# Norm sums partly on GpSimd, and stages that open with four output tiles per operand tile

## The reference, cut to what matters

```python
def modulated_norm(x, g, shift, scale):
    return rms_norm_2(x, g) * (1 + scale) + shift      # x * rsqrt(mean(x^2) + 1e-6) * g
```

```python
def channel_mixer(h, w_up, ffn_dw_w, ffn_dw_b, w_down):
    u = causal_depthwise_conv(h @ w_up, ffn_dw_w, ffn_dw_b)      # 3 taps
    a, b = jnp.split(u, 2, axis=-1)
    return (jax.nn.silu(a) * b) @ w_down
```

## Time and profile before

| | |
|---|---|
| median of 3 runs | 3123.39 us (3120.94 to 3125.38) |
| the profiled execution | 3118.01 us, its span 3116.2 us |
| mean granted TensorE clock | 0.954 of full |
| TensorE busy | 2844.5 us (91%) |
| VectorE, ScalarE busy | 1531.8 us (49%), 1111.8 us (36%) |
| GpSimd busy | 0.2 us |
| DMA | 447.41 MB, mean 144 GB/s |

### The profile page before, as it was taken

One profiled execution on the slowest core, in us unless ns is written; L12 is line 12 of the kernel. 1 busy time (PEld: TensorE's weight loads), 2 busy tenths in 40 slices (PEclk: granted clock), 3 DMA queues, 4 the chain that ended last, 5 costly groups with the idle time before them and its releaser, 6 DMA issues.

```text
span 3116.2 us, 38193 instructions
## 1 busy us (share of the span) xinstructions
PE 2844.5 (91%) x15788; PEld 2328.8 (75%) x15788; DVE 1531.8 (49%) x2262; ACT 1111.8 (36%) x1661; POOL 0.2 (0%) x4
## 2 busy tenths in 40 slices
PE   6887899999868999989999899999989999877998
PEld 4675688997755888977878775787867777655898
DVE  3579636753898357543333423333342323455454
ACT  2444415643444156532222322222232222323443
POOL 0000000000000000000000000000000000000000
PEclk8998899998988999999999999999999999889999
DMA  6541246545421556435353212333225443120553
GB/s 268 195 162 55 75 169 225 214 170 209 157 81 41 189 189 258 170 141 190 121 196 115 81 62 88 128 140 136 105 87 202 151 169 142 68 81 28 189 183 115
DMA packets 122460, 447.41 MB, mean 144 GB/s; under 512 B 13488, under 2 KB 14640, under 8 KB 121904
## 3 DMA queue, kind: packets, MB, share of 16 engines
q1 hardware_dynamic: 122288, 444.97, 39.8%
HBM read 443.87 MB, written 1.05 MB: 143 GB/s over the span
## 4 chain that ended last, share of the span: by engine, by line
PE 78%; DVE 14%; DMA 3%; ACT 3%; issue 1%; SPq 0%; DVEq 0%; ACTq 0%
PE ps L473 21%; PE ps L474 20%; PE ps L475 20%; PE ps L477 17%; DMA ring<-stream 3%; DVE area L1339 3%; DVE area L1515 2%; DVE rests L1263 2%; DVE stat L1370 1%; DVE rs L1302 1%; DVE work L1379 1%; PE ps L637 1%; DVE work L1366 1%; DVE area L1310 1%; ACT heads L925 0%
## 5 line engine op out<-in xcount | busy, mean ns | idle before, releaser
L473 PE MATMUL ps<-h_split,heads 128*128 128x256 f32 (+1 forms) x2992 | 1015.1, 339 | 104.0 <-DVE h_split L1316 60.8
L474 PE MATMUL ps<-h_split,heads 128*128 128x256 f32 (+1 forms) x2992 | 988.6, 330 | 0.0
L475 PE MATMUL ps<-h_split,rests 128*128 128x256 f32 (+1 forms) x2992 | 986.8, 330 | 0.0
L1263 DVE TENSOR_TENSOR rests<-ring,heads 128x1024 fp32r<-128x1024 f32 x520 | 630.2, 1225 | 678.1 <-ACT heads L925 673.2
L925 ACT ACTIVATE heads<-ring 128x1024 fp32r<-128x1024 f32 x520 | 540.6, 1056 | 712.3 <-DMA ring<-stream 370.8
L473 PEld LDWEIGHTS ps<-h_split,heads 128*128 128x128 f32 x2992 | 588.5, 197 | 212.2 <-DVE h_split L1316 69.3
L474 PEld LDWEIGHTS ps<-h_split,heads 128*128 128x128 f32 x2992 | 590.6, 197 | 47.4 <-issue 3.4
L475 PEld LDWEIGHTS ps<-h_split,rests 128*128 128x128 f32 x2992 | 589.1, 197 | 46.1
L473 PE MATMUL ps<-hid_split,heads 128*128 128x256 f32 (+1 forms) x1056 | 365.4, 346 | 0.0
L475 PE MATMUL ps<-hid_split,rests 128*128 128x256 f32 (+1 forms) x1056 | 355.1, 336 | 0.0
L474 PE MATMUL ps<-hid_split,heads 128*128 128x256 f32 (+1 forms) x1056 | 354.8, 336 | 0.0
(11 more groups left out here) (155 smaller groups left out, 2071.4 us busy)
## 6 DMA issues: line engine op xcount, KB each, us to landing
ring<-stream SPq DMA_DIRECT2D x836, 512.0 KB, 3.5
consts<-constants SPq DMA_DIRECT2D x1, 1920.0 KB, 11.3
x_sb<-x_in SPq DMA_DIRECT2D x1, 1024.0 KB, 9.2
x_sb<-ctx_in SPq DMA_DIRECT2D x1, 1024.0 KB, 4.8
out<-area SPq DMA_DIRECT2D x1, 1024.0 KB, 4.8
cols<-columns SPq DMA_DIRECT2D x1, 695.5 KB, 4.1
consts<-constants SPq DMA_DIRECT2D x1, 643.0 KB, 10.3
sg<-positions_in SPq DMA_DIRECT2D x1, 128.0 KB, 10.1
```

The source lines that it names most:

```text
L473: nc.tensor.matmul(out, lhsT[0], rhs[0], start=first, stop=False)
L474: nc.tensor.matmul(out, lhsT[0], rhs[1], start=False, stop=False)
L475: ins = nc.tensor.matmul(out, lhsT[1], rhs[0], start=False, stop=last)
L1263: nc.vector.tensor_tensor(rests[:, u % RING, :], ring[:, u % RING, :], as_f32(heads[:, n % HEADS_RING, :]), ALU.subtract)\
```

## The change

Three things change.

1. GpSimd adds the squares of tiles 1 to 5 of each norm onto tile 0 (`sums`, five additions, each waiting for the one before it). TensorE does three ones-products instead of eight, of the sum and of squares 6 and 7, all after the stage's last output tile.
2. The first four output tiles of `lat`, of each up layer, of `ain` and of `q2` are computed together: four products per k, in four PSUM banks (`linear_quad`). Where a bank held two SEQ tiles, the first four tiles take a bank each (`take_two`), and their readers on ScalarE and VectorE read two banks (`halves_of`). The weight stream is reordered to match (`quad`).
3. In `each_pair` the splits follow the new order: those of pair 2's units stand ahead of `begin(0)`, those of pair 3's units in iteration 0 (on ScalarE between `begin(0)` and `finish(0)`), and iteration 1 has none.

```diff
+SUMMED = KD - 2
@@ weight_blocks
+    def quad(name, n):
+        for k in range(KD):
+            for e in range(4):
+                put(name, k, n + e)
...
             for j in range(lo, hi):
-                pair(up, up_order(width), 2 * j)
+                if lo == 0 and j < 2:
+                    if j == 0:
+                        quad(up, 0)
+                else:
+                    pair(up, up_order(width), 2 * j)
@@ tensor engine
+            def take_two(g):
+
+                if nbank[0] % 2:
+                    nbank[0] += 1
+                b = nbank[0] % BANKS
+                take_bank((*g, "second"), b + 1)
+                take_bank(g, b)
+                nbank[0] += 2
+                return ps[:, b, 0:SEQ], ps[:, b + 1, 0:SEQ]
...
+            def linear_quad(outs, name, n, act, dones, ready):
+
+                for k in range(KD):
+                    ready(k)
+                    for e in range(4):
+                        w, unit = weights(name, k, n + e)
+                        product(outs[e], w, act(k), k == 0, k == KD - 1, dones[e] if k == KD - 1 else None, unit)
...
             def mean_square(p, T_, k):
 
-                if k == 0:
+                if k == SUMMED - 1:
                     for q in last_cols:
 
                         wait_read(q)
                     last_cols[:] = [(p, "ms")]
                     new_banks[(p, "ms")] = COLS_BANK
-                pe.wait_ge(scalar_done, A.at((p, "sq", k)))
-                product(ps[:, COLS_BANK, 0:T_], mat("ones"), squared(T_, k), k == 0, k == KD - 1,
-                        (p, "ms") if k == KD - 1 else None)
-
-            def norm(p, T_, done=0):
-
-                for k in range(done, KD):
+                    pe.wait_ge(pool_done, G.at((p, "sum")))
+                else:
+                    pe.wait_ge(scalar_done, A.at((p, "sq", k)))
+                product(ps[:, COLS_BANK, 0:T_], mat("ones"), squared(T_, 0 if k == SUMMED - 1 else k),
+                        k == SUMMED - 1, k == KD - 1, (p, "ms") if k == KD - 1 else None)
+
+            def norm(p, T_):
+
+                for k in range(SUMMED - 1, KD):
                     mean_square(p, T_, k)
                 return once(lambda k: pe.wait_ge(vector_done, V.at((p, "h", k))))
...
+                def first_pairs():
+                    if shared:
+                        outs = [o for j in range(2) for o in take_two((p, "up", j))]
+                        linear_quad(outs, up, 0, hx, (None, (p, "up", 0), None, (p, "up", 1)), ready)
+                    else:
+                        names = [(p, kind, j) for j in range(2) for kind in kinds]
+                        linear_quad([take_bank(g) for g in names], up, 0, hx, names, ready)
...
                     for j in range(lo, hi):
-                        pair(j, [take_bank((p, kind, j)) for kind in kinds])
+                        if j == 0:
+                            first_pairs()
+                        elif j > 1:
+                            pair(j, [take_bank((p, kind, j)) for kind in kinds])
...
-                        if hi == FJ:
-                            after_down(m)
@@ gpsimd
+            def sums(p, T_):
+
+                for k in range(1, SUMMED):
+                    if k == 1:
+                        pool.wait_ge(scalar_done, A.at((p, "sq", 0)))
+                    pool.wait_ge(scalar_done, A.at((p, "sq", k)))
+                    total = squared(T_, 0)
+                    nc.gpsimd.tensor_tensor(total, total, squared(T_, k), ALU.add)\
+                      .then_inc(pool_done, G.mark((p, "sum") if k == SUMMED - 1 else None))
+                    pool.wait_ge(pool_done, G.n)
@@ scalar engine, each_pair
                     for j in range(lo, hi):
+                        if j == 0:
+                            next_split()
+                            next_split()
                         begin(j)
-                        next_split()
-                        next_split()
+                        if j != 1:
+                            next_split()
+                            next_split()
                         finish(j)
```

More of the change, by code:

```diff
@@ L182, in weight_blocks @@
         if l % 2 == 0:
-            pair("ain", together(range(KD)), 0)
-            linear("ain", KD, range(2, 4))
+            quad("ain", 0)
             linear("uin", KD, range(4))
@@ L380, in bank, with halves_of @@
             return ps[:, bank_of.get(g, 0), :]
+        def halves_of(g, apart):
+            b = bank_of.get(g, 0)
+            return ps[:, b:b + 2, 0:SEQ] if apart else two(ps[:, b, :])
         def as_f32(a):
@@ L573, in hook, with ffn @@
                     pending.append(group)
-            def ffn(p, up, down, T_, ready, after_down):
+            def ffn(p, up, down, T_, ready):
                 shared = T_ == SEQ
@@ L655, in _ @@
                 guests = MIXER_MODS[l]
-                ready = norm((*p, "mix"), SEQ, 0 if l == 0 else KD - 2)
+                ready = norm((*p, "mix"), SEQ)
                 hx = lambda k: h_of(k, slice(0, SEQ))
-                for c in range(3):
-                    out = take_bank((p, "lat", c))
-                    linear(out[:, 0:SEQ], f"lat_{l}", KD, 2 * c, hx, None, ready)
-                    linear(out[:, SEQ:TOK], f"lat_{l}", KD, 2 * c + 1, hx, (p, "lat", c))
+                outs = [o for c in range(2) for o in take_two((p, "lat", c))]
+                linear_quad(outs, f"lat_{l}", 0, hx, (None, (p, "lat", 0), None, (p, "lat", 1)), ready)
+                out = take_bank((p, "lat", 2))
+                linear(out[:, 0:SEQ], f"lat_{l}", KD, 4, hx)
+                linear(out[:, SEQ:TOK], f"lat_{l}", KD, 5, hx, (p, "lat", 2))
                 hook(*guests[0])
@@ L772, in _ @@
                     linear(out[:, 0:SEQ], f"out_{l}", KD, m, lambda k: merged[:, k, :], (p, "out", m))
-                    behind((*p, "ffn"), SEQ)(m)
-                ready = norm((*p, "ffn"), SEQ, KD - 2)
-                ffn((*p, "ffn"), f"up_{l}", f"down_{l}", SEQ, ready,
-                    behind(("b1", 1, "mix"), SEQ) if l == 0 else behind(("b2", 0, "f1"), TOK))
+                ready = norm((*p, "ffn"), SEQ)
+                ffn((*p, "ffn"), f"up_{l}", f"down_{l}", SEQ, ready)
             for l in range(DEPTH):
                 p = ("b2", l)
-                ready = norm((*p, "f1"), TOK, KD - 2)
-                ffn((*p, "f1"), f"f1up_{l}", f"f1down_{l}", TOK, ready, behind((*p, "mix"), TOK))
-                ready = norm((*p, "mix"), TOK, KD - 2)
+                ready = norm((*p, "f1"), TOK)
+                ffn((*p, "f1"), f"f1up_{l}", f"f1down_{l}", TOK, ready)
+                ready = norm((*p, "mix"), TOK)
                 hx = h_of
                 if l % 2 == 0:
-                    linear_pair([take_bank((p, "a", g)) for g in range(2)], "ain", together(range(KD)), 0, hx,
-                                [(p, "a", g) for g in range(2)], ready)
-                    for g in range(2, 4):
-                        linear(take_bank((p, "a", g)), "ain", KD, g, hx, (p, "a", g))
+                    linear_quad([take_bank((p, "a", g)) for g in range(4)], "ain", 0, hx,
+                                [(p, "a", g) for g in range(4)], ready)
                     for g in range(4):
@@ L833, in _ @@
                         linear(take_bank((p, "out", m)), "oab", KD, m, lambda k: mixed[:, k, :], (p, "out", m))
[L834 removed]
                 else:
[L836 removed]
+                    hs = lambda k: h_of(k, slice(0, SEQ))
+                    outs = [o for c in range(2) for o in take_two((p, "q", c))]
+                    linear_quad(outs, "q2", 0, hs, (None, (p, "q", 0), None, (p, "q", 1)), ready)
+                    for c in range(2, 4):
                         out = take_bank((p, "q", c))
[L838 to L839 removed]
+                        linear(out[:, 0:SEQ], "q2", KD, 2 * c, hs)
+                        linear(out[:, SEQ:TOK], "q2", KD, 2 * c + 1, hs, (p, "q", c))
                     for c in range(2):
@@ L876, in _ @@
                         linear(out[:, 0:SEQ], "o2", KD, m, lambda k: attn[:, k, :], (p, "out", m))
-                        behind((*p, "f2"), SEQ)(m)
                 T_ = TOK if l == 0 else SEQ
-                ready = norm((*p, "f2"), T_, KD - 2)
-                ffn((*p, "f2"), f"f2up_{l}", f"f2down_{l}", T_, ready,
-                    behind(("b2", 1, "f1"), TOK) if l == 0 else behind("fin", SEQ))
-            norm("fin", SEQ, KD - 2)
+                ready = norm((*p, "f2"), T_)
+                ffn((*p, "f2"), f"f2up_{l}", f"f2down_{l}", T_, ready)
+            norm("fin", SEQ)
+        @block.gpsimd
+        def _(pool):
+            def sums(p, T_):
[7 more added lines that the diff above has]
+                    pool.wait_ge(pool_done, G.n)
+            for l in range(DEPTH):
+                sums(("b1", l, "mix"), SEQ)
+                sums(("b1", l, "ffn"), SEQ)
+            for l in range(DEPTH):
+                sums(("b2", l, "f1"), TOK)
```

(4 more changed lines are left out.)

48 lines of the change are left out of this document (22 added, 26 removed).

## The result

The changed kernel takes 3098.8 us (median of 4 runs, 3095.1 to 3102.1) against 3122.6 for the kernel before beside it (4 runs, 3120.9 to 3125.4): a ratio of 0.9924, 95% interval 0.9911 to 0.9936, or 23.8 us less. Subtracting the two traces therefore shows only 15.9 of the 23.8 us.

What follows compares the result with a forecast made beforehand. TensorE was taken as the bound, 78% of the chain that ended last. Terms -32.1, -2.5, -8.1, +6.1, +5.7 and +5.2 made 25.7 us less, so the median 3123.4 became 3097.7 us, range 3078 to 3113.

Steps and rivals of the forecast that it cites:

- ones-products: Behind output tiles of ten norms, five products fewer each, 0.43 us in SEQ and 0.85 in TOK: 32.1 us gained.
- quads, five SEQ stages: In `lat` and `up` of both layers and `f2up_1`, four tiles per `h` tile fill TensorE's idle time: 2.5 us gained.
- `q2`: In `q2`, four tiles per k keep TensorE busy and the clock returns sooner: 8.1 us gained, 3.7 if it stays down.
- splits, stall and clock: In `up_0` and `up_1`, moved splits make TensorE stand 6.1 and 5.7 us more, plus 5.2 us for half clock.
- The additions hidden: GpSimd's additions, 0.84 us in SEQ, are covered by output tiles; first norm uncovered: 0, with +1.8 or -4.3 us.
- the fourth rival: GpSimd additions and VectorE's `rests` exclude each other, delaying six norms behind down stages by 42 us: 3140 us, chance 4%.
- The stall: Before the guest's columns, TensorE stands 6.1 us more in `up_0` and 5.7 us more in `up_1`.
- The clock behind it: Behind the stands in `up_0` and `up_1`, 5.2 us of half clock costs 2.6 us each, 5.2 together; bounds 1.7 and 6.3.
- So it isn't repeated: After the stands in `up_0` and `up_1`, ScalarE has a free pair ahead again, so no further stand follows.
- Costless splits: Rival: pair 3's unit lands before ScalarE asks for it, so the moved splits cost nothing: 3080.7 us, chance 18%.
- Costs in all feed-forwards: Rival: copied rows or pair 4's splits come late in the four other feed-forwards too, 6 us each: 3122 us, chance 7%.
- GpSimd as the bound: Rival: the five chained additions outlast six output tiles; gain gone at 4.6 us per SEQ addition, 3147 us at 5; chance 5%.

Runs made afterwards that it cites:

- experiment 2: The kernel before with only GpSimd's sums and three ones-products a norm, matmul order and splits as before: 3093.8 us, ratio 0.9910.
- experiment 4: The changed kernel with `q2` in its old order, one output tile over all k at a time: 3109.2 us, ratio 0.9956.
- experiment 1: The changed kernel with pair 3's two splits back in iteration 1 of each feed-forward: 3081.7 us, ratio 0.9868.
- experiment 7: experiment 1 with three unread additions ahead of each real one, except in the first norm: 3080.4 us, ratio 0.9870.
- experiment 9: The changed kernel with pair 3's splits back in iteration 1, guest's rows copied right behind `begin(j)`, first norm's eight ones-products on TensorE: 3066.7 us, ratio 0.9829.
- experiment 10: experiment 1 with six unread additions ahead of each real one, except in the first norm: 3197.0 us, ratio 1.0240.
- experiment 8: experiment 1 with all eight squares summed by GpSimd, seven additions and one ones-product a norm: 3099.7 us, ratio 0.9931.

## Why the prediction was right

The forecast was 3097.7 us; 3098.8 was measured. The mechanisms were right, but that the time is met within 1.1 us is luck: the errors of the terms cancel. Term by term, each kernel against the kernel before beside it where nothing else is said:

| term | said, us | measured |
|---|---|---|
| ones-products | -32.1 | -27.1 (experiment 2) |
| quads, five SEQ stages | -2.5 | -4.6 (stages of the changed kernel against experiment 2's) |
| `q2` | -8.1 | -7.2 (stage) against before, -8.0 against experiment 4 |
| the two lines above together | -10.6 | -12.1 (experiment 1 against experiment 2) |
| splits, stall and clock | +17.0 | +15.4 (the change against experiment 1; 17.1 between their medians) |
| sum | -25.7 | -23.8 |

The ones-products brought 5.0 less than said, the quads 1.5 more, and the splits cost 1.6 less, each good to 1 or 2 us: in sum the gain is 1.9 too small. Of this the time shows 1.1, as the forecast started from a median of 3123.4 for the kernel before and the one beside the change had 3122.6.

- **Ones-products.** A SEQ product is worth 0.43 as said: `out_0`'s additions lie one bare output tile apart. A TOK one is worth 0.90 rather than 0.85 in the three TOK down stages, each 4.50 us shorter in the trace of experiment 2; behind `down_1` (4.27) and `oab` it is 0.85 to 0.86 as said. That puts the step at about 33. But 0.9 was lost in the first norm, and some 5 us were given back where shorter stages are not what sets the pace. In experiment 2, `up_1` with `down_1` took 0.4 us less than before where 4.3 less was due: TensorE waits 5.8 us for rests where it waited 4.8, 3.7 for rows where it waited 2.0, and works 2.1 us longer at half clock, worth 1.0. `f2up_1` with `f2down_1` took 0.9 us more where 2.1 less was due: the wait for rests, behind a split that waits for its DMA, went from 1.5 to 3.1 us, and the time at half clock from 4.2 to 7.4. So the step that was mis-sized most is this: what is taken from TensorE does not count in full where a wait for the weight stream comes next, because the wait grows. That the transfers might not follow stood among the prediction's signs of being wrong, without a price in the sum.
- **The additions hidden.** Right, 0.76 and 1.29 us on average against 0.84 and 1.7 taken. The ten covered norms have no wait for GpSimd. In the first norm the term said 0 and left out the fourth rival, which is at work there. Here is GpSimd's timeline (the five additions, then the fourth alone), below it VectorE's and TensorE's:

```profile
42.62 4.79 POOL L933 TENSOR_TENSOR sq<-sq 128x256 f32<-128x256 f32 x5 [42.17 <-ACT sq L997]
...
45.03 1.58 POOL L933 TENSOR_TENSOR sq<-sq 128x256 f32<-128x256 f32 x1
```

```profile
44.74 1.29 DVE L1329 TENSOR_TENSOR rests<-ring,heads 128x1024 fp32r<-128x1024 f32 x1 [1.38 <-ACT heads L987]
```

```profile
47.56 2.90 PE L505 MATMUL ps<-sq,consts 128*128 128x256 f32 x6 [4.94 <-POOL sq L933]
```

  The chain ended at 47.4 rather than 46.0: it began at 42.6 rather than 41.8, as everything ahead of it was 0.7 late in this execution, and took 4.8 us rather than 4.2. Four of the additions took 0.72 to 0.73 us; the fourth started while VectorE formed `rests` and took 1.58. That is so in each of the nine traces in which GpSimd adds in this norm. Measured from the last product ahead of it, the root came 0.9 us later than before, and that one addition is 0.86 of it. (The prediction's upper side, +1.8 for additions of 0.42 us, is a slip: 48.91 less 41.8 + 2.1 + 2.6 is 2.4. The lower end of the range, 3078, holds with it: 3080.7 less 2.4 is 3078.3.)
  The Trainium skill (GPSIMD Engine Reference, section "Elementwise — side-by-side cycle accounting") has an addition at 1.96 times VectorE's time, measured there at 2048 columns. The rows give 1.8 at 256 columns (762 ns against the 420 of the earlier trace rows).
- **Quads in SEQ stages.** The direction was right and the size half of what it was. The stages with a quad were 1.4 (`lat_0`), 0.7 (`up_0`), 1.0 (`lat_1`), 0.7 (`up_1`) and 0.8 us (`f2up_1`) shorter than in experiment 2, not 0.5 each. One thing the prediction left out: the clock is back at 1.00 before the last `h` tiles come. In experiment 2 it rises 4.4 us after the first product of `lat_1`, and the seventh step, behind that, still takes 0.67 us where three matmuls at 1.00 take 0.36; idle time there counts in full, not half. The stages behind TOK norms were the same with quads and without (within 0.1 us in experiments 1 and 2), as said, `q2` apart.
- **`q2`.** Right, and by the mechanism said: products without gaps, and the clock back 6.8 us after its fall. The rows of the windows say it, 0.50 to 2714.1 and 1.00 from 2714.3, against 0.50 for 17 us in experiment 4. The Trainium skill (TensorE: Matmul & The Clock Gate, section "Loop structure matters more than you think") wants products back to back and warns of a long wait before every one of them. The trace agrees: 0.50 for 17 us with a wait of some 0.57 us at each `h` tile, and 1.00 again after 6.8 us without.
- **The stall.** The replayed chain was right to a few tenths of a us: from the first split to the columns 15.6 us said, 15.7 measured (493.07 to 508.75). TensorE waits 6.70 in both, against 1.01 and none in the earlier trace rows: 12.4 more, 11.8 said.
- **The clock behind it.** The cost was right, and by luck. The prediction took 5.2 us of half clock at each stand, as behind a norm, worth 5.2 us for both; it lasted 10.0 and 10.2 us. TensorE was busy for 7.15 and 6.82 of these, so each cost half of that, 7.0 for both. But the kernel before had four stretches of 3.4 us at 0.50 around its guests (as experiment 1 has), and the changed kernel has three beside the two long ones. Net it is busy 10.7 us more at half clock there, worth 5.4.
- **"So it isn't repeated".** Half right. No second stand of 6.7 us follows, but the other guests' columns in `up_1` wait 1.99 and 1.98 where they waited 1.01, and 1.43 and 0.98 in experiment 1. Against experiment 1 all waits of TensorE in the two feed-forwards are 13.2 us more, where the prediction has 11.8, and the clock costs 5.4. Together that is 18.6 of the 18.8 us between the traces; the times of the runs show 15.4 to 17.1.
- **The rivals.** Costless splits would have given 3080.7; experiment 1, which makes them so, measured 3081.7, or 39.2 below the kernel before beside it where 42.7 was said. Costs in all feed-forwards: ScalarE's rows keep TensorE waiting in `up_0` and `up_1` alone, apart from the start of the kernel. GpSimd as the bound: the step from hidden to bound lies between 4 and 7 times the real addition, where the prediction had the additions outlast six output tiles from about 4 us for SEQ, five times. The mutual hold exists (below); it is hidden in the ten covered norms and costs 0.86 us in the first.

Left open is what moves single executions by some us where the kernels are the same: from the first modulation rows of a mixer to its `out` stage the first layer took between 358.2 us (experiment 7) and 362.3 (the change), 359.0 before, and the second between 354.6 (experiment 2) and 359.3 (experiment 1), 356.0 before. The waits of TensorE and the stretches of half clock lie differently from trace to trace; why, the runs don't show.

## What to carry to other kernels

In this kernel an idle engine took a reduction off TensorE at no cost, because the last operands stayed with TensorE: give the other engine only what is finished two output tiles before the end, and leave the rest under what follows anyway, here a table load. Where nothing covers the additions, leave them with TensorE (experiment 9). Before a stream's order changes, replay every in-order engine that must follow it: a split that waits for a DMA holds all that is queued behind it on ScalarE, and here it ate some 16 of 40 us. A small copy for which TensorE waits belongs ahead of work that is wanted later; moving it gave 13 us, as much as the quads of all stages (12).

## What the runs showed of the hardware

GpSimd and VectorE do hold each other up. VectorE's `rests` (two operands in SBUF) all take the same time in the trace of before, by tile:

```profile
L1263 DVE TENSOR_TENSOR rests<-ring,heads x520: 1217/1225/1228, 32.4 to 3092.0; 128x1024 fp32r<-128x1024 f32 x174
```

Their longest (third of the three, ns) is 1568 in the kernel after, and 2308 in experiment 10:

```profile
L1329 DVE TENSOR_TENSOR rests<-ring,heads x520: 1217/1226/1568, 33.1 to 3076.5; 128x1024 fp32r<-128x1024 f32 x174
```

```profile
L1334 DVE TENSOR_TENSOR rests<-ring,heads x520: 1215/1225/2308, 32.7 to 3172.9; 128x1024 fp32r<-128x1024 f32 x174
```

In the kernel after, the sum over all 520 is 4 us more (mean 1233 against 1225 ns), and it is hidden, as VectorE is up to four units ahead. The additions grow too. Each of the ten drawn-out additions of experiment 8 started 0.15 to 0.53 us after a `rests`, and ended 0.58 us (256 columns) or 1.12 us (512) behind the end of that `rests`; alone they take 0.73 and 1.27. These stood on the path, as did the one in the first norm of the changed kernel. The Trainium skill (SBUF — State Buffer, section "Who interferes with whom") says that a VectorE instruction with two SBUF inputs contends with a GpSimd instruction that reads SBUF, and calls the pair of ports that they share an exclusive lock. The rows agree: the addition that comes later ends about its own length after the `rests` that was there, and no `rests` grew by more than the 1.3 us of one addition (2308 less 1225 is 1.08).

The half clock was the other surprise. Around and behind stands of 6.70 us it lasted 10 us twice, with TensorE busy for some 70% of them, where the same clock in `q2`, behind a norm, lasted 6.8 us. And waits far shorter than a norm had it behind them: in experiment 1, 3.4 us at 0.50 follow four of the six guests, where TensorE waits 1.98 to 2.69 us for rests and 0.98 to 1.43 for rows; behind the first guests of `up_0` and `up_1`, with waits of the same size, there is none.
